# A decoder block on one core: another order of the first stage, spare banks and moved waits behind it

## The reference

```
mod  = silu(c) @ w_ada + b_ada            # c: one row of 2048; w_ada: 2048 x 12288, 96 MB
sh1, sc1, g1, sh2, sc2, g2 = split(mod, 6)
h    = rms_norm(x, norm1_w) * (1 + sc1) + sh1
proj = h @ w_in                           # 2048 x 7168: q k v gate of 8 retention heads,
                                          #              q k v of 8 difference-attention heads
y_ret = group_norm(retention(rotary(q), rotary(k), v)) * ret_gn_w * silu(gate)
y_dif = rms_norm((softmax(q1 k1) - lam * softmax(q2 k2)) v) * subln_w * (1 - lam_init)
x    = x + g1 * (concat(y_ret, y_dif) @ w_out)
h2   = rms_norm(x, norm2_w) * (1 + sc2) + sh2
x    = x + g2 * (relu(h2 @ w_mlp1)**2 @ w_mlp2)    # 8192 hidden features
out  = rms_norm(x, final_norm_w)
```

## Time and profile before

| | |
|---|---|
| median of 3 runs | 2373.59 us (2372.52 to 2373.86) |
| the profiled execution | 2372.57 us, span 2370.7 us |
| PE, PEld busy | 2312.1 us, 1883.6 us |
| DVE, ACT, POOL busy | 1264.7, 754.5, 77.5 us |
| DMA | 328.25 MB, mean 138 GB/s; in the first two of 40 slices 377 and 402 GB/s |

### The profile page before, as it was taken

The page is one execution under the profiler, slowest core; times in us unless marked ns, Lnnn a source line. Parts: engine busy times, 40 slices in busy tenths (PEclk is TensorE's granted clock), DMA queues, the critical chain, the costliest instruction groups (busy, mean ns, idle before and its releaser), DMA issues.

```text
span 2370.7 us, 28575 instructions
## 1 busy us (share of the span) xinstructions
PE 2312.1 (98%) x10384; PEld 1883.6 (79%) x10384; DVE 1264.7 (53%) x1801; ACT 754.5 (32%) x1025; POOL 77.5 (3%) x59
## 2 busy tenths in 40 slices
PE   4999999999999999999999999999999999999998
PEld 2568888878787788888888888888888888888887
DVE  7977988866666675733333333333333333333354
ACT  3233343344545422421221221221221322222233
POOL 0011110100101000000000000000000000000000
PEclk9999999999999999999999999999999999999999
DMA  9956677622222574232222222222222222222222
GB/s 377 402 205 218 228 269 248 247 95 84 73 87 70 189 274 168 80 107 97 97 93 95 96 97 97 97 97 97 97 94 94 94 97 97 97 97 96 99 89 98
DMA packets 90630, 328.25 MB, mean 138 GB/s; under 512 B 10064, under 2 KB 10576, under 8 KB 89936
## 3 DMA queue, kind: packets, MB, share of 16 engines
q1 hardware_dynamic: 89568, 326.41, 39.3%
q10 hardware_dynamic: 1008, 1.13, 0.1%
HBM read 323.31 MB, written 4.19 MB: 138 GB/s over the span
## 4 chain that ended last, share of the span: by engine, by line
PE 87%; DVE 9%; ACT 2%; issue 1%; DMA 1%; POOL 0%; SPq 0%; POOLq 0%; ACTq 0%; DVEq 0%
PE bank L437 27%; PE bank L438 27%; PE bank L441 27%; DVE ada_sb L1058 3%; DVE w_lo L1051 2%; PE bank L578 1%; DVE prob L1058 1%; PE bank L544 1%; PE bank L461 1%; DMA xy<-x_t 1%; PE bank L569 0%; PE bank L492 0%; DMA prob<-ada 0%; ACT w_hi L757 0%; ACT L850 0%
## 5 line engine op out<-in xcount | busy, mean ns | idle before, releaser
L437 PE MATMUL bank<-act_hi,w_hi 128*128 128x512 f32 (+1 forms) x2112 | 828.8, 393 | 13.1 <-DVE act_lo L1098 4.6
L438 PE MATMUL bank<-act_lo,w_hi 128*128 128x512 f32 (+1 forms) x2112 | 819.9, 389 | 0.0
L757 ACT ACTIVATE w_hi<-raw 128x1024 fp32r<-128x1024 f32 x392 | 413.8, 1056 | 896.0 <-PE bank L441 841.5
L1051 DVE TENSOR_TENSOR w_lo<-raw,w_hi 128x1024 fp32r<-128x1024 f32 x392 | 491.9, 1257 | 308.9 <-ACT w_hi L757 296.0
L441 PE MATMUL bank<-act_hi,w_lo 128*128 128x512 f32 (+1 forms) x2112 | 518.3, 387 | 0.0
L437 PEld LDWEIGHTS bank<-act_hi,w_hi 128*128 128x128 f32 x2112 | 397.8, 188 | 101.5 <-issue 17.7
L438 PEld LDWEIGHTS bank<-act_lo,w_hi 128*128 128x128 f32 x2112 | 397.7, 188 | 81.9 <-issue 1.7
L441 PEld LDWEIGHTS bank<-act_hi,w_lo 128*128 128x128 f32 x2112 | 394.5, 188 | 81.1
L437 PE MATMUL bank<-u_hi,w_hi 128*128 128x512 f32 (+1 forms) x1040 | 401.6, 387 | 0.0
L438 PE MATMUL bank<-u_lo,w_hi 128*128 128x512 f32 (+1 forms) x1040 | 400.2, 386 | 0.0
L1453 DVE SCALAR_TENSOR_TENSOR xy<-bank,modr,xy 128x512 f32 (+1 forms) x141 | 105.9, 751 | 413.2 <-PE bank L441 413.2
(11 more groups left out here) (152 smaller groups left out, 1121.7 us busy)
## 6 DMA issues: line engine op xcount, KB each, us to landing
raw<-weights SPq DMA_DIRECT2D x400, 512.0 KB, 3.2
ada_sb<-ada SPq DMA_DIRECT2D x172, 512.0 KB, 5.4
prob<-ada SPq DMA_DIRECT2D x20, 512.0 KB, 6.7
xy<-x_t SPq DMA_DIRECT2D x16, 512.0 KB, 6.1
out<-rows_out SPq DMA_DIRECT2D x4, 1024.0 KB, 4.8
decay_sb<-decay SPq DMA_DIRECT2D x7, 256.0 KB, 3.1
silu_c<-c_row SPq DMA_DIRECT2D x1, 1024.0 KB, 5.6
rot_sb<-rot ACTq DMA_DIRECT2D x2, 256.0 KB, 7.1
```

The costliest lines, as they stand in the source:

```text
L437: pe.matmul(acc, stationary, hi, start=first, stop=False)
L438: pe.matmul(acc, stationary, lo, start=False, stop=False)
L757: nc.scalar.activation(w_hi[:, w], raw[:, r], ACT.Copy).then_inc(hi_ready, 1)
L1051: nc.vector.tensor_tensor(w_lo[:, w], raw[:, r], w_hi[:, w].bitcast(F32), ALU.subtract).then_inc(lo_ready, 1)
```

## The change

- **c as one row.** ACT issues c (8 KB, one partition). PE spreads it over the partitions with four products by a row of ones into banks 0 to 3 (`spread_c`), and ACT takes the silu in four pieces between the squares. SP begins with x.
- **The sum of squares.** All 16 squares have a place of their own in `rows_out`, so ACT waits for no sum. DVE adds 13 of them (`first_square_sums`, 12 additions), PE sums tiles 8, 10 and 12 itself (`first_sums`).
- **Dots of whole rows.** One DVE instruction of 128 x 2048 in place of two of 128 x 1024; it starts from the bias, so only one small operation (`scale1`) is left. Rings: `NADA_1` = 3 and `NADA` = 2 whole rows (as many bytes). The first tile's two rows come as halves (`half_dot`). The half dots of its shift row wait until POOL has done the power. The heads' dots are whole too (`modulation_rest`), and `modulation_sum` adds the bias alone.
- **Single k tiles.** No groups: `normed`, one dot, the split, one dot, `scale1`. `normed(0, 0)` reads the spread roots in PSUM.
- **Tile 15 is split**, with a `first_done` for each of banks 0 to 6, so that `rotate_q` and the gates start before the chunk ends. `first_chunk` takes all hi by hi products first and waits for `act_lo` after them. Head 1's first two chunks take the odd tiles' `act_lo` as they come, and its attention slots come one later.
- **SP's order.** The rotary tables and the decay come behind chunk `FIRST` (before: from ACT's queue during the squares); the lambdas and the mask behind chunk 1.
- **One table.** ACT loads the silu set, later a set with Ln and Exp in it, by explicit instructions.
- **Behind the first stage.** ACT splits y(0), y(1) before it takes the last v; `finish_dif` of the last head is one slot earlier; tile 4 of the output projection goes to bank 4 (`SPARE_OUT`), the fifth up tile to bank 6 (`SPARE_UP`); for the second norm PE sums the last square itself and does `token_sums` and `token_spread` within a chunk.
- **The end.** `last_sums` goes ahead of the last transposes; rows are scaled and written in halves (eight DMAs of 512 KB).

```diff
-NADA = 4
-NADA_1 = 6
+NADA = 2
+NADA_1 = 3
-WHOLE = tuple(range(1, KT, 2))
+WHOLE = tuple(range(1, KT - 1, 2))
+PE_SQUARES = (8, 10, 12)
...
@@ SP
-            sp.dma_start(silu_c[:], c.partition_broadcast(P128)).then_inc(c_landed, 16)
             for p in range(KT // 2):
                 sp.dma_start(xy[:, 2 * p:2 * p + 2], ...)
             for k in range(KT):
+                if k == 0:
+                    for i in range(4):
+                        load_ada_half(i)
+                else:
+                    for e in range(2):
+                        load_ada(Count(2 * k + e))
+                load_raw(Count(k))
...
             load_raw(Count(FIRST))
+            sp.dma_start(rot_sb[:, 0], rot[0, 0]).then_inc(rot_landed, 16)
+            sp.dma_start(rot_sb[:, 1], rot[0, 1]).then_inc(rot_landed, 16)
+            sp.dma_start(decay_sb[:], decay[0]).then_inc(decay_landed, 16)
...
@@ PE
+            def first_chunk(k):
+                pe.wait_ge(act_hi_ready, k + 1)
+                for i in range(BLOCKS):
+                    product(i, w_hi, act_hi, start=k == 0)
+                pe.wait_ge(act_ready, SPLIT.index(k) + 1)
+                if k < KT - 1:
+                    ...
+                else:
+                    pe.wait_ge(lo_ready, made(Count(k)))
+                    for i in range(BLOCKS):
+                        product(i, w_hi, act_lo)
+                        product(i, w_lo, act_hi, stop=True).then_inc(*((first_done, 1) if i < BLOCKS - 1 else (chunk_done, 1)))
+            def spread_c():
+                pe.wait_ge(c_landed, 16)
+                for i in range(4):
+                    pe.matmul(bank[i][:], ones[0:1], silu_c[0:1, i * TOK:(i + 1) * TOK], start=True, stop=True)
...
+        tile_chunk(Count(C_OUT + 8 * g + 2 * t + half), SPARE_OUT if (g, t) == (1, 0) else t, half)
...
-            tile_part(Count(last), 7, 0, 1, chunk_done)
-            token_sums(2)
-            tile_part(Count(last + 1), 7, 1, 1, chunk_done)
-            token_spread(2)
+            tile_part(Count(last), 7, 0, 1, chunk_done, lambda: token_sums(2))
+            tile_part(Count(last + 1), 7, 1, 1, chunk_done, lambda: token_spread(2), BLOCKS // 2)
...
+            last_sums(0)
             turn_part(KT - 1, 0, KT)
-            last_sums(0)
             down_part(7, s0 + 31, 1, chunk_done)
             turn_part(KT - 2, 1, KT + 1)
+            last_sums(1)
             turn_part(KT - 1, 1, KT + 2)
-            last_sums(1)
@@ ACT
             for m in range(KT):
                 square_x(m, (x_landed[m // 2], 16))
+                if m % 2 == 1 and m < 8:
+                    i = m // 2
+                    act.wait_ge(c_spread, i + 1)
+                    nc.scalar.activation(silu_c[:, i * TOK:(i + 1) * TOK], bank[i][:], ACT.Silu).then_inc(silu_ready, 1)
...
+            load_table(LN_EXP_SET)
...
-            take_v(NRET + NDIF - 1, Count(C_OUT))
+            act.wait_ge(chunk_done, C_OUT - 1)
             split_y(0)
             split_y(1)
+            take_v(NRET + NDIF - 1, Count(C_OUT))
@@ DVE
+            def dot_ada(a, to, start=0.0):
+                nc.vector.tensor_tensor_reduce(ada_at(r), ada_at(r), silu_c[:], 1.0, start, ALU.mult, ALU.add, to)
...
+            half_dot(0, 0)
+            half_dot(0, 1)
+            scale1(0)
+            token_mean(1)
+            dve.wait_ge(tok_r_ready, 1)
+            half_dot(1, 0)
+            half_dot(1, 1)
+            for k in range(KT):
+                normed(0, k)
+                if k == 0:
+                    rest_w(Count(0))
+                    modulated_rest(0, 0)
+                if k + 1 < KT:
+                    dot1(k + 1, 0)
+                if k in SPLIT and k > 0:
+                    rest_w(Count(k))
+                    modulated_rest(0, k)
+                if k + 1 < KT:
+                    dot1(k + 1, 1)
+                    scale1(k + 1)
...
+            for k in WHOLE[:2]:
+                whole_rest(k)
+            rotate_q(0, Count(FIRST), False)
+            for k in WHOLE[2:4]:
+                whole_rest(k)
             rest_w(Count(FIRST))
```

More of the change, by code:

```diff
@@ L375, in load_phase @@
                     load_raw(s0 + (j + 2))
-                    for _ in range(2 * slots[j]):
+                    for _ in range(slots[j]):
                         load_ada(ada_phase(h) + part)
@@ L451, in first_chunk, with product @@
             def first_chunk(k):
-                split_products([(i, bank[i][:], act_hi[:, k], act_lo[:, k], k == 0, k == KT - 1,
-                                 (act_ready, SPLIT.index(k) + 1) if i == 0 else None) for i in range(BLOCKS)], Count(k))
+                w = w_place(Count(k))
+                def product(i, weight, moving, start=False, stop=False):
+                    return pe.matmul(bank[i][:], weight[:, w, i * P128:(i + 1) * P128], moving[:, k], start=start, stop=stop)
+                pe.wait_ge(hi_ready, made(Count(k)))
@@ new lines, in spread_c, with first_sums @@
+            def spread_c():
+                pe.wait_ge(c_landed, 16)
+                for i in range(4):
+                    pe.matmul(bank[i][:], ones[0:1], silu_c[0:1, i * TOK:(i + 1) * TOK], start=True, stop=True)\
+                        .then_inc(c_spread, 1)
+            def first_sums():
+                for n, m in enumerate(PE_SQUARES + (None,)):
+                    if m is None:
+                        pe.wait_ge(ssq_ready, FIRST_SUMS)
+                    else:
+                        pe.wait_ge(sq_ready, m + 1)
+                    for tb in range(TB):
+                        tokens = slice(tb * P128, (tb + 1) * P128)
+                        mm = pe.matmul(ps_a[:, tb:tb + 1], ssq[:, tokens] if m is None else square_at(m)[:, tokens], inv_d[:],
+                                       start=n == 0 and tb == 0, stop=m is None, skip_group_check=True)
+                mm.then_inc(mean_done, 1)
@@ L470, in quad_chunk, with tile_part, pairs, quad_part @@
                                 for i in range(BLOCKS)], s)
-            def tile_part(s, b, half, part, done):
+            def tile_part(s, b, half, part, done, between=None, at=BLOCKS):
                 cols = half_tokens(part)
[L475 to L479, removed]
+                def pairs(blocks):
+                    return [(i, bank[b][:, cols], act_hi[:, 8 * half + i, cols], act_lo[:, 8 * half + i, cols],
+                             half == 0 and i == 0, half == 1 and i == BLOCKS - 1, None) for i in blocks]
+                w = w_place(s)
+                pe.wait_ge(hi_ready, made(s))
+                for i, acc, hi, lo, first, _, _ in pairs(range(BLOCKS)):
+                    if i == at:
+                        between()
+                    stationary = w_hi[:, w, i * P128:(i + 1) * P128]
+                    pe.matmul(acc, stationary, hi, start=first, stop=False)
+                    pe.matmul(acc, stationary, lo, start=False, stop=False)
+                if between is not None and at == BLOCKS:
+                    between()
+                pe.wait_ge(lo_ready, made(s))
+                for i, acc, hi, _, _, last, _ in pairs(range(BLOCKS)):
+                    mm = pe.matmul(acc, w_lo[:, w, i * P128:(i + 1) * P128], hi, start=False, stop=last)
+                if done is not None:
+                    mm.then_inc(done, 1)
+            def quad_part(s, j, part, between, done, early=None):
                 cols, w = half_tokens(part), w_place(s)
```

411 lines of the change are left out of this document (220 added, 191 removed).

## The result

The changed kernel takes **2358.49 us** (median of 4 runs, 2358.26 to 2359.54), the kernel before 2373.06 beside it. The ratio is 0.994, 95% interval 0.9925 to 0.9956: faster by 14.6 us, where 27.0 were forecast, and outside the range given. The profiled execution took 2359.54 us with a span of 2357.7, so span against span it is 13.0 us.

A forecast was written before the change was run, and what follows sets the result against it. PE's matmuls were taken to bound the kernel, with DVE leading the first stage and DMA and PE within 0.5 us; nine terms summed to 27.0 us, from 2373.59 to 2346.6 us, likeliest range 2340 to 2355.

The forecast's parts named there:

- first stage, start included: From PE's start to the first stage's end: 13.6 us less, between 10.5 and 16.5, ending at 128.8 us.
- behind tile 15, gates: Just behind the first stage: PE's wait and slow chunk go, 4.3 us, and 0.2 us of idle at the gates.
- table loads in the heads: In the heads, two idle times of 0.54 us behind ACT's table loads go with one table: 1.1 us.
- y waits and spare bank out: At the output projection: waits for y(0), y(1) and y(15) go, 2.9 us, and for bank 0's residual, 1.0 us.
- second norm: PE's wait for the second norm's first tiles, 1.70 us, goes, plus 0.5 guessed for smaller waits: 2.2 us.
- spare bank up: At the fifth up tile, a spare bank removes PE's idle time of 0.73 us: 0.7 us.
- The pace: In the first stage, DVE's work sets a pair of k tiles at 12.6 us, where it was 13.1.
- rival A: First stage: the load through three whole-row buffers sets the pace, 13.5 us a pair, 6.3 us lost, 2353 us; chance 0.10.
- They all fit: Behind tile 15, DVE's queued w_lo and whole_rest fit beside the rotation, so PE has no idle time nor clock fall: 4.3 us.
- Nothing; the cover is PE's row of chunks: In the heads, whole-row dots take 5 us off DVE, which PE does not wait for there: no gain counted.
- Dots: On DVE, a whole-row dot takes 2.21 us, not above 2.30.
- D, the heads starve: Heads: with a two-row ring, landings over 9.9 us stop DVE, then PE; 32 us, 2379 us; chance 0.02.

The follow-up runs named there:

- e4: The changed kernel with a first-stage ring of four whole rows in place of three, and ACT's and DVE's work for chunk FIRST+1 moved up: 2347.15 us.
- e1: The changed kernel with ACT's rounding for chunk FIRST+1 ahead of the gates, k and table load, and DVE's w_lo ahead of k's rotation: 2351.47 us.
- e7: e4 with two table loads put back into each head's root on ACT, between Ln and Exp and behind Exp: 2350.65 us.
- e6: e4 with each row's dot in the heads done as two dots of half rows: 2347.49 us.
- e9: e4 with the dots done by half rows in the heads 5 to 7 alone: 2345.63 us.
- e10: e4 with the old order at the output's start put back, ACT taking the last v before it splits y(0) and y(1): 2348.00 us.
- e5: e1 with a first-stage ring of two whole rows in place of three: 2376.25 us.
- e12: The changed kernel with each whole row loaded by four DMAs of 256 KB, each for 64 partitions, all waited for together: 2440.49 us.

## Why the prediction was wrong, point by point

Forecast and measured, in us. The measured column compares, in the spans of before and after, the stage's ends and behind them the starts of ACT's rounding of the same chunk:

| step | forecast | after | what the runs add |
|---|---|---|---|
| start of PE | 8.2 | 8.2 | |
| first stage, start included | 13.6 | 7.7 | 13.9 with a ring of four (e4) |
| behind tile 15, gates | 4.5 | -3.0 | 6.4 to 6.9 back with ACT's order (e1, e4) |
| table loads in the heads | 1.1 | 0.5 | 2.2 by itself (e7), less sq_lo waits of 1.7 (e6, e9) |
| y waits and spare bank out | 3.9 | 4.6 | 1.5 needs table and order (e7, e10) |
| second norm | 2.2 | 2.0 | |
| spare bank up | 0.7 | 0.4 | |
| the end | 1.0 | 0.8 | |
| sum | 27.0 | 13.0 | |

- **The pace was the first wrong step.** The forecast had a pair at 12.6 us and rival A, the load sets the pace through the three-row ring, at 0.10. A happened, and as it was written: 13.5 us a pair. Its reason "against" failed at one number: it took 5.4 us for a landing "while the queue was full" from part 6 of the profile's page. That is a median over the whole kernel, most of it in heads where the queue is quiet, and it is a half row's, set against a need for whole rows. Counted between 26 and 125 us, half rows of the kernel before landed in 6.5 us:
```profile
ada_sb<-ada SPq DMA_DIRECT2D x39, 512.0 KB, 6.5
```
  A turn of three rows in 3/4 x 12.6 = 9.45 us leaves 9.45 - 2.35 = 7.1 us for a landing; whole rows needed 7.6. The size of A's loss was right (7 x 0.9 = 6.3, measured 5.9). With four rows the stage gains 13.9 us for 13.6, but it is PE that sets its pace then, at 12.7 to 12.85 us a pair, and not DVE, which the forecast had in the lead.
- **"They all fit" was the second, and the larger.** Behind tile 15 the forecast followed bank 0, the rotation of q and DVE's queue, and found no idle time for chunk FIRST, which is right. It did not walk ACT's queue to the next `w_hi`: the rounding for FIRST+1 stood behind a wait for DVE, five gates, k's rotation and the table load. Before the change the same queue had 2.4 us of PE's wait, a slow chunk of 7.3 us and head 0's scores in front of PE's need, and was never last. That is a new wait in the place of a removed one, and the clock's fall came back with it: 7.5 us off the forecast, 6.4 to 6.9 of it given back by the order alone (`e1`, `e4`).
- **The table loads** had a mis-sized term in both directions: taking them out is worth 3.5 us in all (`e7`), 2.2 of it in the heads, and 1.7 us of that was taken back by POOL, which whole-row dots hold up. "Nothing; the cover is PE's row of chunks" counted DVE's time and not that of the engine beside it.
- **Dots**: a whole-row dot took 2.27 from start to start, against 2.21 forecast and a bound of 2.30. Right within the bounds.
- **Start, second norm, spare bank up, end**: right within 0.3 us each. The y waits and the spare bank out brought 4.6 us for 3.9, but the 1.5 of them that the forecast put down to the order alone needed the one table as well.
- **D, the heads starve**, did not happen: DVE waited 0.9 us in all for rows there. `e5` shows its mechanism in the first stage, where a turn has no 10 us: two rows cost 24.8 us. `e12` shows it in the heads.
- **The 358 GB/s of the Trainium skill**, which the prediction cites, were rightly set aside: `e4` ran at 409 GB/s between 76 and 104 us.

With both places mended the kernel gains 25.4 us from span to span (`e4`), against 27.0.

## What to carry to other kernels

Fewer and larger buffers in a ring are not the same ring: write down its turn (use, and landing from the issue on) with the landing time of the busy stretch itself, not of the whole kernel, and compare it with the need. When a wait is removed, walk every engine's queue one chunk further than the wait, each instruction with its duration, to the next thing that PE needs. Ask too what else covered that thing, and whether the change moves it. And a longer instruction on DVE can have a price on POOL, also when DVE has time to spare.

## What the hardware showed that was not expected

- The more rows are under way, the longer each takes to land: 5.6, 7.6 and 9.9 us for a 1 MB row with two, three and four of them, at 325, 382 and 407 GB/s.
- Four DMAs of 64 partitions moved 242 GB/s, four of 128 partitions 375, both at a DMA share of 1.03; the kernel took 79 us more with the first.
- POOL's 128x512 subtraction took 2.60 us beside DVE's dots of 2048 columns and 1.55 beside dots of 1024: in both it was done 1.14 to 1.15 us after the dot had ended. DVE's next subtraction took 2.30 us in place of 1.22.
